# Four gate buffers, an interleaved first pair of tiles in the second output projection, and a later slot for one norm's mean, in a two-block transformer kernel

## The reference, cut to what matters

```python
# first block (end of it)
h = x + mixed @ w_out
nm = rmsnorm(h, mlp_norm_g)                  # the "second norm": phase "mlp"
h = h + square(relu(nm @ w_ff1)) @ w_ff2
x = rmsnorm(h, final_norm_g)
# second block (hybrid_layer)
proj = rms_norm(x, norm1_g) @ w_in
q_sb, k_sb, v_sb, q_hg, f_hg, i_hg, g_hg, gate_sb, gate_hg = split(proj)
y_sb = stick_breaking_attention(...) @ w_branch[:512]
y_hg = hgrn2_mixer(...) @ w_branch[512:]
mixed = sigmoid(gate_sb) * y_sb + sigmoid(gate_hg) * y_hg
h = x + mixed @ w_out
h = h + (silu(hn @ w_gate) * (hn @ w_up)) @ w_down
```

## Time and profile before

| | us |
|---|---|
| median of 3 runs | 1405.07 |
| lowest and highest | 1404.99, 1407.67 |
| the profiled execution, its own time | 1408.77 |
| its span, first to last instruction | 1407.2 |
| PE busy in it | 1384.1 (98%) |
| ACT, DVE, POOL busy | 834.8, 624.3, 210.9 |
| mean granted TensorE clock | 0.999 |

### The profile page before, as it was taken

How to read it: one execution, slowest core, us unless ns; L and a number is a source line. 1 busy time by engine, 2 the same in 40 slices (tenths; PEclk the granted TensorE clock), 3 DMA queues, 4 the chain that set the end, 5 groups by cost and what they waited for, 6 DMA issues and landing times.

```text
span 1407.2 us, 17461 instructions
## 1 busy us (share of the span) xinstructions
PE 1384.1 (98%) x6784; PEld 1119.2 (80%) x6784; DVE 624.3 (44%) x1216; ACT 834.8 (59%) x1240; POOL 210.9 (15%) x259
## 2 busy tenths in 40 slices
PE   9999999999999999999999999999999999999999
PEld 6977966788888888887867778877788888888887
DVE  6055365521211212357488889954534322341232
ACT  5574575654644545665477767665557645663661
POOL 0210000111111111111211111111111111111110
PEclk9999999999999999999999999999999999999999
DMA  7975644698888888876755656789888989889875
GB/s 226 247 170 131 143 117 95 149 211 189 195 192 198 190 195 190 192 166 127 154 130 112 144 141 153 179 215 262 207 189 195 190 193 199 190 189 198 195 167 123
DMA packets 72791, 247.99 MB, mean 176 GB/s; under 512 B 8099, under 2 KB 8115, under 8 KB 72581
## 3 DMA queue, kind: packets, MB, share of 16 engines
q0 software_dynamic: 36144, 130.32, 51.0%
q1 hardware_dynamic: 35844, 114.95, 25.5%
q10 hardware_dynamic: 720, 1.61, 0.3%
HBM read 240.52 MB, written 6.32 MB: 175 GB/s over the span
## 4 chain that ended last, share of the span: by engine, by line
PE 79%; DVE 9%; ACT 7%; issue 3%; DMA 3%; DVEq 0%; ACTq 0%
PE bank L474 24%; PE bank L478 24%; PE bank L481 24%; ACT WH L780 1%; DVE eb L1426 1%; DMA RAW<-in_w_out 1%; PE bank L589 1%; PE bank L632 1%; PE bank L608 1%; PE bank L622 1%; ACT WL L788 1%; DMA gates<-hs 1%; DVE eb L1422 1%; ACT eb L934 1%; DMA WH<-in_w_in 1%
## 5 line engine op out<-in xcount | busy, mean ns | idle before, releaser
L474 PE MATMUL bank<-NH,WH 128*128 128x512 f32 x1152 | 466.6, 406 | 7.1 <-ACT NH L885 5.3
L478 PE MATMUL bank<-NL,WH 128*128 128x512 f32 x1152 | 449.3, 391 | 0.8 <-DVE NL L1170 0.5
L481 PE MATMUL bank<-NH,WL 128*128 128x512 f32 x1152 | 448.9, 391 | 0.0
L780 ACT ACTIVATE WH<-RAW 128x1024 fp32r<-128x1024 f32 (+2 forms) x195 | 201.7, 1035 | 205.4 <-PE bank L481 184.8
L474 PEld LDWEIGHTS bank<-NH,WH 128*128 128x128 f32 x1152 | 217.2, 189 | 72.0 <-issue 29.9
L478 PEld LDWEIGHTS bank<-NL,WH 128*128 128x128 f32 x1152 | 217.4, 189 | 47.3 <-issue 3.8
L481 PEld LDWEIGHTS bank<-NH,WL 128*128 128x128 f32 x1152 | 216.9, 188 | 46.0
L788 ACT ACTIVATE WL<-WH 128x1024 fp32r<-128x1024 f32 (+2 forms) x219 | 229.3, 1048 | 15.3 <-DMA WH<-in_w_in 10.1
L478 PE MATMUL bank<-AL,WH 128*128 128x512 f32 x432 | 168.2, 389 | 0.0
L481 PE MATMUL bank<-AH,WL 128*128 128x512 f32 x432 | 168.1, 389 | 0.0
L474 PE MATMUL bank<-AH,WH 128*128 128x512 f32 x432 | 168.1, 389 | 0.0
(11 more groups left out here) (289 smaller groups left out, 1655.2 us busy)
## 6 DMA issues: line engine op xcount, KB each, us to landing
RAW<-in_w_ff SPq DMA_DIRECT2D x64, 512.0 KB, 6.1
WL<-in_w_ff POOLq DMA_DIRECT2D x64, 512.0 KB, 8.7
WL<-in_w_in POOLq DMA_DIRECT2D x62, 512.0 KB, 7.4
RAW<-in_w_gu SPq DMA_DIRECT2D x44, 512.0 KB, 6.4
WL<-in_w_gu POOLq DMA_DIRECT2D x44, 512.0 KB, 8.7
RAW<-in_w_in SPq DMA_DIRECT2D x32, 512.0 KB, 7.0
WH<-in_w_in POOLq DMA_DIRECT2D x32, 512.0 KB, 7.1
RAW<-in_w_down SPq DMA_DIRECT2D x20, 512.0 KB, 5.0
```

Of the source, the lines that this page charges most:

```text
L474: e.matmul(o, a[0], a[1], start=(k == 0), stop=False)
L478: e.matmul(o, b[0], b[1], start=False, stop=False)
L481: mm = e.matmul(o, c[0], c[1], start=False, stop=(k == t.kt - 1))
L780: e.activation(WH[p % HL][:, 0:n], RAW[raw_slot[p]][:, 0:n], ACT.Copy).then_inc(*act.sig("high", p))
```

## The change

Three edits. The gates on their way to HBM get four buffers, `hs` and two more, `hs_`, at rows 25 and 26 of the memory plan (row 25 is also `gw[9]`, so the transfer back of gate 9 waits for the transfer out of gate 14). The first two tiles of `wo2` go into one `together` group, so that they run side by side along the rows as the very first two tiles do; both count as ending at about the same v. And the mean of the second norm is due 7.3 instead of 6 after the start of `f1`, behind row 7 of the first tile.

```diff
@@ Plan.__init__
+        paired = {0, next(u for u, unit in enumerate(units) if unit[0] == "wo2")}
...
-                if u == 0 and c:
-
-                    first = self.together[0][0]
+                if u in paired and c:
+
+                    first = self.together[-1][0]
                     t.v0, first.v1 = first.v0, v - 1
-                    self.together[0].append(t)
+                    self.together[-1].append(t)
@@ build_program
+        top[0] = mark + 25 * S * 4
+        hs4 = hs + two("hs_", 2)
...
-        mean_time = {"attn": 24.0, "mlp": plan.start(("f1", 0)) + 6, "ffn": plan.start(("gu", 0)) + 6}
+        mean_time = {"attn": 24.0, "mlp": plan.start(("f1", 0)) + 7.3, "ffn": plan.start(("gu", 0)) + 6}
@@ scalar(), gate_sigmoids
-                    u = t.i % 2
+                    u, n = t.i % 2, t.i % 4
                     yield due(t, 2.0)
-                    back = [(f"gate_out{u}", t.i - 2)] if t.i >= 2 else [*stick_end, ("gate", "hg", 2 + u)]
-                    sigmoid_act(("gs", t.i), gx[u], hs[u], freed(t), *back)
+                    back = [(f"gate_out{n}", t.i - 4)] if t.i >= 4 else [*stick_end, ("gate", "hg", 2 + u)]
+                    sigmoid_act(("gs", t.i), gx[u], hs4[n], freed(t), *back)
                     yield due(t, 7.0)
-                    sigmoid_exp(("gs", t.i), hs[u])
+                    sigmoid_exp(("gs", t.i), hs4[n])
@@ vector(), gate_sigmoids
-                    sigmoid_dve(("gs", t.i), gx[u], hs[u])
+                    sigmoid_dve(("gs", t.i), gx[u], hs4[t.i % 4])
@@ sync(), gates_out and gates_in
-                    e.dma_start(gates[t.i], hs[t.i % 2]).then_inc(*sp.sig(f"gate_out{t.i % 2}", t.i, by=16))
+                    e.dma_start(gates[t.i], hs4[t.i % 4]).then_inc(*sp.sig(f"gate_out{t.i % 4}", t.i, by=16))
...
-                    sp.wait_ge((f"gate_out{n % 2}", n))
+                    sp.wait_ge((f"gate_out{n % 4}", n))
...
+                        if n == 9:
+                            sp.wait_ge(("gate_out2", 14))
```

## The result

| | before | after |
|---|---|---|
| median, 12 runs each | 1404.87 us | 1402.07 us |
| lowest, highest | 1403.24, 1407.67 | 1400.67, 1407.11 |
| ratio, 95% interval | | 0.9981 [0.9974, 0.9989] |
| profiled execution, own time and span | 1408.77, 1407.2 | 1403.49, 1402.1 |

The change makes the kernel 2.7 us faster (by the ratio, on 1404.87), with an interval from 1.5 to 3.7 us. The two profiled executions are 5.1 us of span apart, nearly the forecast 5.3; that this is not the gain is the main thing to learn here.

A forecast was written before the change was run, and what follows sets the result against it. PE was taken as the bound, busy 1384.1 of 1407.2 us. Four buffers and pair 4.6 plus mean 0.7 made 5.3 us, taken from the median 1405.07: 1399.8, range 1397.0 to 1403.4.

The forecast's parts named there:

- Four buffers, mechanism: Before br0: ACT's Abs of g14 waits only for its gx; PE's gap falls to 0.8 us, clock stays 1.00.
- Four buffers, size: At br0: Abs starts at 943.6 instead of 947.83; suppliers run 4.1 us earlier, PE in full stride 5.5 us earlier.
- What is late next: From br1 to wo2: waits for B7's low part and tile 6's bank; 0.3 us taken off for O0's landing.
- a stall of 0.3: In br1: PE waits 0.3 us for B7's low part, landing at 984.1 and needed at 983.8.
- stall of 2.3 us: At wo2's second matmul: PE waits 2.3 us for the bank of br1's tile 6, replacing the row stall.
- The row stall of 2.2: At row 7 of the first wo2 tile: a loss of 2.2 us before the change, which the pair covers.
- The pair: At wo2: alternating banks cost PE nothing, 0.227 us per matmul; gain with the four buffers 4.9, taken as 4.6 us.
- The mean: At the second norm: row 7's matmuls fill PE's wait before the mean; gain 0.68 us, from nothing to 0.7.
- (a): Rival: the DMA engines are the limit and O0 lands nearly as before; gain 1.5 us, 1403.6; 10%.
- (c): Rival: the clock falls in the 2.3 us wait at the wo2 pair, 1.8 lost; gain 3.5, 1401.6; 10%.
- (d): Rival: the clock stays at the lower level through the whole wo2 pair; 4.5 us slower, 1409.6; 3%.
- (e): Rival: before br0 ACT isn't freed, the Abs of g14 still waits; 1403.4; 4%.

The follow-up runs named there:

- e5b: The full change measured a second time, against the kernel before: ratio 0.9978 [0.9969, 0.9986].
- e11: As e6b, and ACT splits raw piece O0 behind its first mh copy (due 6 v later); ratio to the kernel before 0.9959 [0.9946, 0.9972], median 1399.21 us.
- e9: The kernel before, unchanged, for a second profile of it: execution 1406.31 us.
- e3: The kernel before with only the mean's later place (7.3): ratio to the kernel before 1.0001 [0.9992, 1.0009].
- e10: The kernel before, unchanged, for a third profile of it: execution 1407.27 us.
- e1: The kernel before with only the four gate buffers: ratio to the kernel before 0.9992 [0.9983, 1.0001].
- e4: The full change without the pair (four buffers and the mean): ratio to the kernel before 0.9987 [0.9978, 0.9995].
- e12: As e11, without the pair: ratio to the kernel before 0.9960 [0.9948, 0.9972].
- e6b: The full change, with SP issuing B7's raw piece sooner (due 5.1 v earlier): ratio to the kernel before 0.9968 [0.9956, 0.9979].
- e7b: As e6b, and gates 8 to 15 come back 4 to 10 v later: ratio to the kernel before 0.9968 [0.9956, 0.9980].
- e8b: The full change without bringing gates 10 to 15 back, so the computation differs: ratio to the kernel before 0.9963 [0.9949, 0.9976].
- e2: The kernel before with only the first two wo2 tiles side by side: ratio to the kernel before 0.9997 [0.9988, 1.0007].

## Why the prediction was right or wrong

The direction was right and 1402.07 lies in the range; the size was not: 5.3 us forecast, 2.7 and 3.1 measured. Step by step:

- **Four buffers, mechanism**: right in each part. ACT freed behind `gx`, a gap of 0.87 for 0.8 in all nine profiles that have the buffers, the nine matmuls in 2.6 us at full clock for "2.04 plus about 0.4". That the clock would hold was argued from a row that does not show it (last section).
- **Four buffers, size: this step failed.** The start "at 943.6 instead of 947.83" and the 5.5 us built on it took one execution's 10.72 us for the kernel's. That transfer, which the change takes out of the path, took 7.6 to 12.3 us in the profiles. Its mean over the 14 is 9.5, so a usual gap is 9.5 - 5.8 = 3.7, and the term (3.7 - 0.9) + (3.9 - 2.6) = 4.1 instead of 5.5. The profiled execution stood 3.7 us above the median; the forecast noted it and still took its whole gain from the median. So the term that was mis-sized is the gap before `br0`, 4.9 us for a usual 3.7.
- **What is late next**: the sum was about right, its place was not. "a stall of 0.3" at B7 was 3.2 us in the profile of after and none in e5b, the same kernel; the "stall of 2.3 us" at the bank was 0 and 1.2, the 0 only because B7 had already held PE back (an estimated 2.9 otherwise). The rest takes 56.1 and 54.1, on average 2.7 over the ideal 52.4; forecast 2.6, and 0.3 for O0. Its cause, ACT in front of O0, was right (e11).
- **The row stall of 2.2** was oversized in the same way: in the four profiles without buffers or pair (e9, e3, before, e10) the rest is 1.4 over the ideal on average. The stage then gains 4.1 - (2.7 - 1.4) = 2.8 us, where the forecast had 4.6.
- **The pair**: no cost of alternating banks, as the earlier trace rows said: two matmuls took 0.46 and 0.45 us in after and e11. The brief idling between groups that the Trainium skill (TensorE: Matmul & The Clock Gate, "A second HAM failure mode: psum-queue depth-cycling") reports of cycling through banks did not appear here. With the lag, the profile of e5b with the pair (rest 54.1) is 1.1 us shorter than e1 and e4 without it (55.2 each), which the times don't resolve; without the lag it is worth nothing (e11, e12).
- **The mean**: its 0.7 us is in the profile and below what the medians resolve. With it the stage's 2.8 makes 3.5, still over 2.7 and 3.1 but inside their intervals' upper part; the remaining 0.4 to 0.8 us is not explained. The same account gives 2.7 for e1 and 3.4 for e4, where 1.1 and 1.8 were measured, just outside their intervals; for e6b, e7b, e8b, e11 and e12 it gives 5.0, 4.5, 6.0, 6.0 and 6.0 against 4.5, 4.5, 5.2, 5.8 and 5.6. It puts the versions in the right order and is up to 1.6 us too high.
- **Rivals**: (a), full DMA engines, holds in part for B7 only: its raw transfer took 7.8 to 10.7 us in the five profiles without the buffers and 11.5 to 13.6 in the four that have them and issue B7 and the gates as the change does. O0's took 12.3 to 13.6 and 12.2 to 14.5, so it did move forward with its request. (c) and (d) did not occur: the clock held after 3.24 and 1.18 us of wait. (e) did not occur.

## What to carry to other kernels

A wait for a DMA is a sample, not a constant: before it is priced, look at a few executions. Here the profiled one was 3.7 us above the median; its gap was 1.2 us over the usual 3.7, its row stall 0.8 over the average and its wait at 720 us 1.35 over the commonest value, which makes most of it. The execution's own time doesn't replace the other profiles, though: e9, with the shortest gap of all, is also above the median of its group (1406.31 for 1405.08). Two late suppliers of one engine need not add: in after the wait for B7 hid most of what PE would have waited at the bank. When a stage speeds up, follow the supply order of the next pieces of weights, and ask which engine stands in order in front of one that isn't needed yet: moving that one split behind more urgent work (e11) took the lag away, where holding back other transfers (e7b) only moved the wait to the next piece.

## What was not expected of the hardware

The clock fell after short gaps and held after longer ones. Before `br0`, gaps of 1.8 to 6.5 us each came with about 3 us of matmuls at the lower level (1.2 GHz), in e9, e2 and e3 beginning about 1 us after PE had restarted; the gap of 0.87 us came with none in nine profiles. Windows of e9:

```profile
949.70:951.40 1.70, 0.11 (x1) 0.00 (x0) 0.03 (x1) 1.70 (x4) 0.81 (x1) 1.00 0.64 152
951.50:953.00 1.50, 1.34 (x3) 0.87 (x4) 1.50 (x3) 1.50 (x4) 0.00 (x0) 0.75 0.77 261
953.00:954.50 1.50, 1.50 (x5) 1.17 (x4) 1.50 (x4) 1.46 (x3) 0.00 (x0) 0.50 1.02 171
```

But 3.24 us in `br1` of after (985 to 988 above) cost nothing, nor did the 2.20 us at 720 in the profile of before. The earlier trace rows do not show the latter: their window ends at 721.00, and PE starts again at 721.67. A window behind it does:

```profile
723.00:725.00 2.00, 2.00 (x14) 1.74 (x13) 2.00 (x7) 2.00 (x6) 0.00 (x0) 1.00 0.00 0
```

In e9, the same kernel, the wait at the same place was shorter, and the clock fell behind it; first PE's timeline, then a window:

```profile
722.51 0.88 PE L608 MATMUL bank<-wT,vS 128*64 128x128 f32 x12 [1.77 <-ACT wT L919]
```
```profile
723.60:725.00 1.40, 1.40 (x4) 1.01 (x4) 1.40 (x5) 1.40 (x3) 0.00 (x0) 0.50 0.03 12
```

The length of a gap alone does not tell what the clock will do, so the forecast's argument from the 2.20 us was right by luck as much as by reason. No run here separates what else decides.
